# Expert stage of a transformer block: two fixed experts loaded early, and another deal of the second block's work

## The reference

```python
p_group = softmax(t @ wg + bg);  p_top_g, g_idx = top_k(p_group, 1)
e_logits = take_along(einsum('td,gde->tge', t, we) + be, g_idx)
p_top_e, e_idx = top_k(softmax(e_logits), 2)
w_sel = p_top_g * p_top_e / sum(p_top_e)
for gi in range(4):                    # only the two chosen experts of a token have a combine that isn't 0
    hid = silu(t @ w_gate[gi]) * (t @ w_up[gi]) * combine[:, gi]
    out += hid @ w_down[gi]
```

## Time and profile before

| | us |
|---|---|
| Median of 3 runs | 1671.16 |
| Lowest and highest | 1663.08, 1674.93 |
| Profiled execution | 1670.68 |
| Its span | 1668.8 |
| PE busy | 1529.8 |
| DVE busy | 487.9 |
| ACT busy | 336.2 |

### The profile page before, as it was taken

One profiled execution on the slowest core, in us unless ns is written; L12 is line 12 of the kernel. 1 busy time (PEld: TensorE's weight loads), 2 busy tenths in 40 slices (PEclk: granted clock), 3 DMA queues, 4 the chain that ended last, 5 costly groups with the idle time before them and its releaser, 6 DMA issues.

```text
span 1668.8 us, 21989 instructions
## 1 busy us (share of the span) xinstructions
PE 1529.8 (92%) x9293; PEld 1047.2 (63%) x9293; DVE 487.9 (29%) x1233; ACT 336.2 (20%) x690; POOL 4.1 (0%) x8
## 2 busy tenths in 40 slices
PE   6999999999799889978989998969889999999897
PEld 3655689888774334634456644548666675888665
DVE  2200086423342311223113000028342232022471
ACT  2311151211212102021200000023212222021461
POOL 0000000000000000000000000000000000000000
PEclk9999999999799799999999999989899999999998
DMA  9989642131269889999999999942122313423100
GB/s 375 408 349 371 237 154 78 51 131 75 104 273 421 344 359 415 391 418 419 419 402 414 406 403 422 368 174 89 64 98 105 151 51 151 152 69 145 51 1 26
DMA packets 54304, 397.59 MB, mean 238 GB/s; under 512 B 6359, under 2 KB 13688, under 8 KB 16440
## 3 DMA queue, kind: packets, MB, share of 16 engines
q1 hardware_dynamic: 40384, 341.85, 51.0%
q10 hardware_dynamic: 13240, 52.16, 7.9%
q0 software_dynamic: 576, 2.10, 0.4%
HBM read 389.80 MB, written 6.29 MB: 237 GB/s over the span
## 4 chain that ended last, share of the span: by engine, by line
PE 80%; DMA 9%; DVE 4%; ACT 3%; issue 2%; SPq 1%; ACTq 1%; DVEq 0%; POOL 0%; POOLq 0%; PEldq 0%; PEld 0%
PE bank L692 16%; PE bank L1435 13%; PE bank L1450 9%; PE bank L2366 7%; DMA work<-in_moe_w_up 4%; PE bank L2383 4%; PE bank L1555 3%; PE bank L1550 3%; PE bank L526 3%; PE bank L2352 2%; PE bank L723 2%; PE bank L1146 2%; PE bank L1160 2%; DMA work<-in_ab_pool_w 1%; DMA work<-in_moe_w_gate 1%
## 5 line engine op out<-in xcount | busy, mean ns | idle before, releaser
L692 PE MATMUL bank<-H,ring 128*128 128x256 f32 (+1 forms) x960 | 245.2, 412 | 1.0 <-ACTq L297 0.7
L692 PEld LDWEIGHTS bank<-H,ring 128*128 128x128 f32 x960 | 181.4, 191 | 52.8 <-issue 28.8
L2366 PE MATMUL bank<-ring,work 128*32 128x512 f32 (+1 forms) x768 | 137.6, 630 | 15.8 <-DMA ring<-in_moe_w_up 5.7
L1435 PE MATMUL bank<-H,work 128*128 128x256 f32 x512 | 115.8, 385 | 0.4 <-issue 0.4
L1435 PE MATMUL bank<-H,ring 128*128 128x256 f32 x512 | 113.4, 381 | 0.0
L1435 PEld LDWEIGHTS bank<-H,work 128*128 128x128 f32 x512 | 97.1, 192 | 19.6 <-issue 6.5
L1435 PEld LDWEIGHTS bank<-H,ring 128*128 128x128 f32 x512 | 97.9, 192 | 13.6
L2366 PEld LDWEIGHTS bank<-ring,work 128*32 128x32 f32 (+1 forms) x768 | 36.3, 122 | 103.9 <-issue 84.8
L1450 PE MATMUL bank<-work,H 128*128 128x512 f32 x192 | 85.2, 596 | 0.0
L1450 PE MATMUL bank<-ring,H 128*128 128x512 f32 x192 | 83.4, 593 | 0.0
L2383 PE MATMUL bank<-ring,work 128*32 128x512 f32 (+1 forms) x384 | 68.0, 624 | 4.1 <-issue 2.2
(11 more groups left out here) (426 smaller groups left out, 1937.9 us busy)
## 6 DMA issues: line engine op xcount, KB each, us to landing
ring<-in_moe_w_gate SPq DMA_DIRECT2D x48, 1024.0 KB, 10.6
ring<-in_moe_w_up SPq DMA_DIRECT2D x48, 1024.0 KB, 9.0
ring<-in_moe_w_down SPq DMA_DIRECT2D x48, 1024.0 KB, 12.1
work<-in_ab_w_in ACTq DMA_DIRECT2D x28, 1024.0 KB, 10.0
ring<-in_ab_w_in SPq DMA_DIRECT2D x14, 2048.0 KB, 7.6
work<-in_ada_w SPq DMA_DIRECT2D x12, 2048.0 KB, 14.9
ring<-in_w_in SPq DMA_DIRECT2D x12, 2048.0 KB, 10.2
work<-in_w_mod SPq DMA_DIRECT2D x12, 2048.0 KB, 9.4
```

Source lines behind the costliest of these rows:

```text
L692: mm = nc.tensor.matmul(tile_bank(i)[:, 0:n], weight(c, k, j * P, (j + 1) * P), rhs(k), start=(k == 0), stop=(k == kt - 1))
L1435: mm = nc.tensor.matmul(b[:, j * T:(j + 1) * T], w_k(m, n, k, at, at + P), H[:, k, m.s], start=(k == 0), stop=(k == DT - 1), skip_group_ch ...
L2366: mm = nc.tensor.matmul(bank[b][rows, :], gath[:, k, rows], half_slot[(load_at[n + half] + e) % NHALF][:, (k % 4) * 512:(k % 4 + 1) * 512] ...
```

## The change

Experts 0 and 1 get their own pass, the first, whatever their rank; it has two experts. Then come the six passes of four (ranks 8 to 31) and three passes of two (ranks 2 to 7). To that end the key by which experts are ranked gets a large number for experts 0 and 1. As their numbers are known, SP loads the two halves of `gate` and of `up` of both (eight halves of 1 MB) in `fixed_sync`, behind the last load of the first block, as the ring slots come free; `sparse_sync` starts with `down` of pass 0.

The pick and gather of pass 0 move into the router, into banks 6 and 7, while `head_pe` and `head_act` go; the query turns are now the first of the body (116 turns in all). `start` goes. `project` and `down` have gaps inside their steps: 0 to 6 in `gate` and `up` (after every second of the eight k tiles of each, but not after the last of `up`), 7 behind the next gather, 8 behind the transposes, 9 to 12 in `down`. The table `TURNS` says how many turns each gap of each pass gets: 5, 17, 19, 13, 23, 15, 12, 2, 2 and 2 per pass; 6 are left behind the last. DVE does the turns of gaps 0 to 6 ahead of the product of the pass, ACT those of 0 to 2 ahead of SiLU and of 3 to 6 ahead of the gather's low half.

`pool_late_dve` computes the means in turns 5 to 8 from the start of `PU` in place of 9 to 12. On DVE the gates of the context are interleaved with the convolutions in another order. The recurrences of the context stay as they were, one direction behind the other.

The diff, cut to its core:

```diff
 N_WIDE = 8
+N_FIXED = 2
+PASSES = [(0, N_FIXED)] + [(N_WIDE + 4 * i, 4) for i in range((NX - N_WIDE) // 4)] + [(2 * i, 2) for i in range(N_FIXED // 2, N_WIDE // 2)]
+FIXED_KEY = 65536.0
...
+    key_no = np.arange(NX) - FIXED_KEY * np.maximum(N_FIXED - np.arange(NX), 0)
...
 
             no = turns["dve_a"]
             a_seen(NPOOL)
-            for _ in range(8):
+            for _ in range(4):
                 yield
             for g in range(NPOOL):
                 pool_mean_dve(dve, chain, m, g, no + g + 1)
-                if g:
-                    mixed_group_dve(dve, m, g - 1)
                 yield
-            mixed_group_dve(dve, m, NPOOL - 1)
-            marks["mixed", m.hf] = turns["dve_d"]
             yield
+            for g in range(NPOOL):
+                mixed_group_dve(dve, m, g)
+                if g == NPOOL - 1:
+                    marks["mixed", m.hf] = turns["dve_d"]
+                yield
 
...
+        def gather_pe(b):
+
+            for k in range(DT):
+                for t in range(TT):
+                    mm = nc.tensor.matmul(bank[b[k // 4]][:, (k % 4) * P:(k % 4 + 1) * P], hrows[:, t, k * P:(k + 1) * P], pick[:, t, :],
+                                          start=(t == 0), stop=(t == 1), skip_group_check=True)
+                if k % 4 == 3:
+                    mm.then_inc(gath_mm, 1)
+
+        def take_low_act(act, p, b):
+            act.wait_ge(gath_mm, 2 * p + 1)
+            nc.scalar.copy(gath[:, 0:4, :].rearrange("p k s -> p (k s)"), bank[b[0]][:]).then_inc(gath_out, 1)
+
+        def take_high_dve(dve, p, b):
+            dve.wait_ge(gath_mm, 2 * p + 2)
+            nc.vector.tensor_copy(gath[:, 4:8, :].rearrange("p k s -> p (k s)"), bank[b[1]][:]).then_inc(gath_out, 1)
+
+        def pass_slots(p, x):
+
+            first, experts = PASSES[p]
+            w = P // experts
+            return x.rearrange("p t (e w) -> p t e w", e=experts), [P, TT, experts, w], first, experts, w
+
+        def make_pick(p, at):
+            o, shape, first, experts, w = pass_slots(p, pick)
+            nc.vector.tensor_tensor(o, bc(slot_no[:, 0:w].unsqueeze(1).unsqueeze(1), shape), bc(at[:, :, first:first + experts].unsqueeze(3), shape),
+                                    ALU.is_equal).then_inc(pick_ready, 1)
+
...
-            next(head)
+            gates_pe(pe, mixers[0])
...
-            next(head)
+            pe.wait_ge(pick_ready, 1)
+            gather_pe(FIRST_GATHER)
 
             pe.wait_ge(lane_out, 3)
             for t in range(TT):
                 mm = nc.tensor.transpose(bank[2][0:2 * NX, t * P:(t + 1) * P], by_expert[:, t, :], ident[:])
             mm.then_inc(lane_mm, 1)
-            next(head)
             pe.wait_ge(lane_out, 4)
...
-            head = head_act(act)
-            for _ in head:
-                pass
+            gate_in_act(act, mixers[0])
+            take_low_act(act, 0, FIRST_GATHER)
...
+            L(V.tensor_scalar(fixed_at, by_expert[:, :, 0:N_FIXED], -1.0, None, ALU.add))
+            make_pick(0, fixed_at)
...
+            if isinstance(e, int):
+                return w[e, :, half * HALF:(half + 1) * HALF]
...
+        FIXED_STEPS = NHALF // N_FIXED
+
+        def fixed_sync(sp):
+            at = 0
+            for n in range(FIXED_STEPS):
+                w, half = (wg, wu)[n // 2], n % 2
+                for i in range(N_FIXED):
+                    displaced = before_moe[at // 2] if at < 2 * RING else early_last[0]
+                    if at % 2 == 0 and displaced is not None:
+                        sp.wait_ge(*last_use[displaced])
+                    sp.dma_start(half_slot[at], half_src(w, i, half)).then_inc(step_in[n], 16)
+                    at += 1
...
         def sparse_sync(sp):
             for p, (first, experts) in enumerate(PASSES):
-                e = [sp.value_load(ids[0:1, first + i:first + i + 1], min_val=0, max_val=NX - 1) for i in range(experts)]
+                e = list(range(N_FIXED)) if p == 0 else [sp.value_load(ids[0:1, first + i:first + i + 1], min_val=0, max_val=NX - 1) for i in range(experts)]
                 for j, w in enumerate((wg, wu, wd)):
                     for half in range(2):
                         n = 6 * p + 2 * j + half
+                        if n < FIXED_STEPS:
+                            continue
...
-        FILL_FOUR, FILL_TWO = (2, 2, 2, 2, 2, 2, 2, 1, 1), (0, 0, 0, 1, 0, 1, 0, 0, 0)
-
-        def fill(body, p, i):
-
-            for _ in range((FILL_FOUR if PASSES[p][1] == 4 else FILL_TWO)[i]):
-                next(body, None)
-
-        def start(body):
-
-            for _ in range(4):
+        TURNS = ((0, 1, 0, 1, 0, 0, 0, 1, 1, 0, 1, 0, 0),
+                 (1, 1, 1, 1, 1, 0, 1, 1, 2, 2, 2, 2, 2),
+                 (2, 2, 2, 2, 3, 1, 1, 1, 1, 0, 1, 2, 1),
+                 (1, 1, 1, 1, 1, 0, 1, 1, 1, 1, 1, 1, 2),
+                 (2, 2, 2, 2, 2, 2, 2, 2, 3, 2, 0, 1, 1),
+                 (1, 2, 0, 1, 1, 1, 1, 1, 1, 1, 2, 2, 1),
+                 (1, 1, 1, 1, 1, 0, 1, 1, 1, 1, 1, 1, 1),
+                 (0, 0, 0, 0, 0, 0, 0, 1, 0, 0, 1, 0, 0),
+                 (0, 0, 0, 0, 0, 0, 0, 1, 0, 0, 1, 0, 0),
+                 (0, 0, 0, 0, 0, 0, 0, 1, 0, 0, 1, 0, 0))
+        assert len(TURNS) == NPASS
+
+        def fill(body, p, *slots):
+
+            for _ in range(sum(TURNS[p][i] for i in slots)):
                 next(body, None)
...
-                    mm.then_inc(step_used, 1)
-                    if at + half < 3:
-                        fill(body, p, at + half)
+                        if k % 4 == 3:
+                            mm.then_inc(step_used, 1)
+                        if k % 2 == 1 and at + k // 2 < 7:
+                            fill(body, p, at + k // 2)
 
...
-                    mm.then_inc(step_used, 1)
-                    fill(body, p, 5 + half)
-
-            gather(0)
-            start(body)
+                        if f % 2 == 1:
+                            mm.then_inc(step_used, 1)
+                        fill(body, p, 9 + f)
+
...
-                project(p, 1, 6 * p + 2, 2)
+                project(p, 1, 6 * p + 2, 4)
                 if p < NPASS - 1:
                     gather(p + 1)
-                fill(body, p, 3)
+                fill(body, p, 7)
                 pe.wait_ge(hid_out, p + 1)
...
-                fill(body, p, 4)
+                fill(body, p, 8)
                 if p < NPASS - 1:
                     pe.wait_ge(gath_out, 2 * p + 4)
                 pe.wait_ge(phid_t_out, p + 1)
                 down(p, 6 * p + 4)
-                fill(body, p, 7)
-                fill(body, p, 8)
             finish(body)
 
         def sparse_act(act, body):
...
+            make_pick(1, place)
             for p in range(NPASS):
-                for i in (0, 1, 2):
-                    fill(body, p, i)
+                fill(body, p, 0, 1, 2, 3, 4, 5, 6)
                 dve.wait_ge(step_used, 6 * p + 4)
                 dve.wait_ge(silu_out, p + 1)
                 nc.vector.tensor_tensor(phid, psig, bank[1][:], ALU.mult).then_inc(hid_out, 1)
                 if p == NPASS - 1:
                     nc.vector.sem_inc(moe_ring_free, 1)
                 else:
-                    take_gathered(p + 1)
-                fill(body, p, 3)
+                    take_high_dve(dve, p + 1, GATHER)
...
         def body_pe(pe):
             m = mixers[0]
+            yield from tiles_pe(pe, m, Q[0])
             yield from tiles_pe(pe, m, K[0])
             yield from rows_pe(pe, m, V[0])
             yield from gate_cols_pe(pe, m)
...
-            conv_dve(dve, chain, m, 0)
-            yield
-            gate_scan_dve(dve, chain, m)
-            conv_dve(dve, chain, m, 1)
-            yield
-            gate_max_dve(dve, chain, m)
-            conv_dve(dve, chain, m, 2)
-            yield
-            gate_arg_dve(dve, chain, m)
-            yield
-            conv_dve(dve, chain, m, 3)
+            for c, gates in enumerate((gate_scan_dve, gate_max_dve, gate_arg_dve, None)):
+                yield
+                conv_dve(dve, chain, m, c)
+                if gates is not None:
+                    gates(dve, chain, m)
+                yield
             a_seen(2)
...
                 load_chunk(sp, c)
                 loads_sync(sp, c)
+            fixed_sync(sp)
             moe_sync(sp)
```

113 lines of the change are left out of this document (37 added, 76 removed).

## The result

The changed kernel takes 1721.9 us (four runs, 1717.0 to 1727.3), the kernel before 1673.1 beside it (1663.1 to 1679.8). The ratio is 1.0298, 95% interval 1.0233 to 1.0362. The prediction was 1684 with a range of 1655 to 1708: the sign was right for the forecast, the size was not, and the result lies outside even the bad case (C, 1707). The profiled execution took 1727.26 us, span 1725.1.

A forecast was written before the change was run, and what follows sets the result against it. DMA was taken as the bound from 462 to 1066 us (busy 0.96), with PE close to full. Terms -20 + 10 + 8 - 9.3 - 4.5 - 6 + 8 + 12 + 13 + 2 = +13 on 1670.7 gave 1684 us, range 1655 to 1708.

The forecast's parts named there:

- Rival C: Clearly slower: turns inside steps, pass 4 and the pool all at their upper ends, +36, 1707 us; chance 0.17.
- Step 1: Two experts loaded early, during the output projection: 20.0 us of DMA leave the full stretch, -20.
- Step 2: Routing without the head: first expert step at about 468, nothing issued until about 472, DMA idles 10 us, +10.
- Step 3: Pass 0 with two experts: +8 new idle; old idle of 485 to 500 us goes, -9.3, and of 545 to 555, -4.5.
- Step 4: Thirteen gaps: shorter stretches to `down` in passes 1, 2, 3 and 6, -6; turns inside steps hold halves longer, +8.
- Step 5: Pass 4: 28.5 us from used `up` to used `down` against 10 to 20 us of DMA work, +12.
- Step 6: Pool means four turns earlier: PE stalls in pass 5 for a product behind the table of inverse counts, +13.
- Step 7: Tail: six turns instead of four left behind the last pass, +2.

The follow-up runs named there:

- Experiment 4: Changed kernel with the fixed experts' eight halves issued behind the routing instead of behind the output projection: 1719.6 us, ratio 1.0304 to the kernel before.
- experiment 5: Changed kernel with both the old deal of turns and VectorE's old pool order: 1684.3 us, ratio 1.0081 to the kernel before.
- 7: Changed kernel with the old deal of turns, but part of each pass's turns moved inside the half-steps: 1699.4 us, ratio 1.0172 to the kernel before.
- 2: Changed kernel with the old deal of turns, new pool order kept: 1685.9 us, ratio 1.0101 to the kernel before.
- 13: The 1651.4 us hand-dealt kernel with part of each gap's turns put inside the half-step ahead of it: 1665.4 us, ratio 0.9975 to the kernel before.
- 8: Changed kernel with old pool order and hand deal: one turn in pass 0, short stretches from used `up` to used `down`, none inside half-steps: 1651.4 us, ratio 0.9886.
- experiment 1: Changed kernel with VectorE's old pool order (eight empty turns ahead of the means): 1708.1 us, ratio 1.0226 to the kernel before.
- 3: Changed kernel with every turn inside a half-step moved to the gap behind it: 1688.4 us, ratio 1.0107 to the kernel before.
- experiment 15: Changed kernel with all turns moved out of half-steps (1688.4 us), plus passes 1 and 4 dealt anew with short stretches: 1677.9 us, ratio 1.0068.
- 12: Changed kernel with only the turns of passes 1 and 4 dealt anew, turns inside half-steps kept: 1717.7 us, ratio 1.0283 to the kernel before.
- 6: Kernel before with nothing but VectorE's new pool order: 1670.4 us, ratio 1.0004.
- 17: Changed kernel, new pool order kept, with only its table of turns replaced by that of the 1651.4 us hand-dealt kernel: 1654.6 us, ratio 0.9895.

## Why the prediction was wrong, step by step

- *Step 1, −20 for the early loads: right as far as it went.* The shares ahead of the stage rose as said, and the column chain kept its 27.88 us. Experiment 4 shows that in this deal the 20 us are worth nothing, since steps 2 and 3 eat them. And they weren't 20 to begin with: DMA's busy time behind 462 us fell by 10 us only, at 2.60 us a MB instead of 2.56 (in experiment 5 it fell by 18, at 2.58). Why a MB takes longer is not shown.
- *Step 2, +10: right*: 12.4 us of idle in 462 to 482 against 1.0 before; PE starts at 465.4 as against 468.
- *Step 3: its +8 and −9.3 held together, its −4.5 was the failure.* Up to 512 us steps 2 and 3 have +10 + 8 − 9.3 = +8.7; the idle went from 10.2 to 17.6 us, +7.4. The −4.5 booked the idle of 545 to 555 as gone with the old pass 0. But it belonged to the first recurrence, and that only came a pass later: there DMA idles 11.6 us (573 to 589). In experiment 5, where steps 1, 2, 3 and 7 alone are at work, the sum says −20 + 10 + 8 − 13.8 + 2 = −13.8 us. Measured: +13.5. These 27 us are three quarters of the 36 that the forecast missed (13 against 49). In its trace 14 of them are this place (+9.7 us of idle for −4.5), 10 are idle behind it (25.9 against 16.1), for which the sum had no term, and 2 are the loads that took less with them. What makes the 10 is not shown.
- *Step 4, −6 and +8.* The −6 was wrong: I had the stretch fall from 21 to below 18 us in four passes. It is 27.1 in pass 1, 14.9 and 18.7 in passes 2 and 3, 19.9 in pass 6, with 11.6 us of idle in the first and 10 in the other three together. In pass 1 I counted turns by their length, and left out that the gate columns wait for ACT and that the recurrence opens with 4.8 us of its own. The +8 for turns inside half-steps was low: 12 to 15 us in two deals (7 against 2, 13 against 8), some 20 between experiments 1 and 3, where more turns stood inside; the bounds were 0 to 20.
- *Step 5, +12: the stretch (28.7 us, 28.5 counted) and the idle (10.7 us) are there, their worth is not shown to be 12.* Passes 1 and 4 together gave 7 to 11 us in experiment 15, not clear of noise, and nothing that can be measured in 12.
- *Step 6, +13: right*, 12 us of idle and 12 us by experiment 1, PE's stall 9.3 us plus 2 for the slow turn. By experiments 5, 6 and 17 it hangs only on which turn stands ahead of the product. The table landed 19.3 us after issue beside SP's queue. That agrees with what the Trainium skill says of queues taken in turn packet by packet (DMA: Bandwidth & Descriptors, "Queues, rings and completion order"): in 880 to 910 us the second hardware queue had as many packets as SP's (1184 against 1164) and moved 1.57 MB against 8.45.
- *Step 7, +2: right.*
- Deal and pool order together (steps 4 to 6) were +27 in the sum; the changed kernel less experiment 5 is 0.0217, 36 us.
- *The range.* Rival C's bounds were those of the new places only. That a term with a minus sign could come out at nothing, or be given back a pass later, was in no case; with +13.8 and +6 added, C would have ended at 1727. The frame was right: DMA sets the end, since the last load lands 45 us later and PE's last `down` ends 46 later. Of the 34 us by which that landing missed the sum (+11 without the tail), 23 are idle (54 against the 31 of the sum's terms) and 10 are busy time that did not leave (10 against 20).

Open: the effects do not add up. Short stretches are worth 25 to 29 us in the kernel with pass 0 short and 4 in the kernel before. The same edit in passes 1 and 4 gave 7 to 11 us without turns inside steps and 3 with them, but these two can't be told apart within the noise. That a share of this lies in where the recurrence's short turns fall is argued, not shown.

## What to carry to other kernels

Where two engines are both near full and a ring two steps deep stands between them, cost each edit by when its steps give their buffers back, not by its share of the time: keep between the last use of one load group and the first of the next as little as can be, and nothing inside a step that holds a buffer. In these runs moving loads out of a full stretch paid only where the consumer also sped up behind them (nothing with five turns in pass 0, 6 to 7 us with one), so a first pass cut in half wants its filler work cut as well. An idle that the trace shows belongs to the work that stands there: before it is booked as a gain, find where that work goes.

## What the runs showed of the hardware

What a stall of PE costs in clock did not follow its length. The granted clock (the column ahead of the DMA share) around a wait of 7.47 us in the changed kernel, behind one of 3.15, and in and behind one of 3.93:
```profile
544.00:548.60 4.60, 0.00 (x0) 0.00 (x0) 0.00 (x0) 0.00 (x0) 0.00 (x0) 0.76 1.01 420
548.60:550.60 2.00, 1.98 (x12) 0.60 (x16) 0.00 (x0) 0.00 (x0) 0.00 (x0) 0.50 1.01 422
...
1113.00:1116.00 3.00, 3.00 (x8) 0.97 (x10) 0.00 (x0) 0.00 (x0) 0.00 (x0) 0.50 1.01 418
...
1039.30:1043.30 4.00, 0.07 (x4) 0.03 (x2) 0.00 (x0) 0.00 (x0) 0.00 (x0) 1.00 1.00 397
1043.30:1046.80 3.50, 3.50 (x16) 1.03 (x16) 0.00 (x0) 0.00 (x0) 0.00 (x0) 1.00 1.02 424
```
In the first two, the clock stands at 0.50 (1.2 GHz) behind the wait; the windows from 553 and from 1116 us have 0.96 and 0.93. In the third it never fell, and the half-step behind it took its usual 3.65 us. Behind the wait of 7.47 us half a half-step took 3.6 instead of 1.9 us and the turn after it 4.2 instead of 3.6, 2.3 us together; behind the wait of 3.15 a half-step took 5.34 instead of 3.65, 1.7 us. Before the change it was 2.9 us behind a wait of 3.73. The changed kernel has 15 waits for weights instead of 8, and not each of them paid this.
